# Depthwise convolution taps moved from TensorE to ScalarE and GpSimd in a two-layer decoder trunk

## What is computed

```
u = h @ w_in + b_in                       # 2048 -> 4096
a, gate = split(u)
u = a * sigmoid(gate)
u = causal depthwise convolution of u, 31 taps per channel, + b_dw
u = silu(layer_norm(u, ln_g, ln_b))
return u @ w_out + b_out
```

## Time and profile before

| | us |
|---|---|
| median of 3 runs | 2216.86 (2216.32 to 2218.45) |
| the profiled execution's own time | 2215.75 |
| its span in the trace | 2214.0 |
| TensorE busy | 2192.6 (99%) |
| VectorE busy | 1417.3 (64%) |
| ScalarE busy | 1006.6 (45%) |
| GpSimd busy | 208.1 (9%) |
| mean granted TensorE clock | 0.998 |

### The profile page before, as it was taken

The page is one execution under the profiler, slowest core; times in us unless marked ns, Lnnn a source line. Parts: engine busy times, 40 slices in busy tenths (PEclk is TensorE's granted clock), DMA queues, the critical chain, the costliest instruction groups (busy, mean ns, idle before and its releaser), DMA issues.

```text
span 2214.0 us, 32918 instructions
## 1 busy us (share of the span) xinstructions
PE 2192.6 (99%) x13136; PEld 1945.1 (88%) x13136; DVE 1417.3 (64%) x1319; ACT 1006.6 (45%) x890; POOL 208.1 (9%) x125
## 2 busy tenths in 40 slices
PE   8999899999999999999999999999999999999998
PEld 8999788888888888888888898888888888888887
DVE  7999877555555554556767667775565556555655
ACT  7665645443344433444444444444443344433444
POOL 7999100000000000000000000000000000000000
PEclk9999999999999999999999999999999999999999
DMA  9665354546554555455454435555555554555462
GB/s 238 169 175 166 117 207 171 209 171 209 189 190 171 208 189 196 171 209 190 172 172 142 143 115 204 186 204 175 202 173 206 175 204 174 206 190 190 172 212 77
DMA packets 250048, 400.54 MB, mean 181 GB/s; under 512 B 6407, under 2 KB 72143, under 8 KB 249935
## 3 DMA queue, kind: packets, MB, share of 16 engines
q1 hardware_dynamic: 249406, 398.74, 53.3%
q0 software_dynamic: 352, 0.56, 0.1%
q10 hardware_dynamic: 208, 0.07, 0.0%
HBM read 397.24 MB, written 2.10 MB: 180 GB/s over the span
## 4 chain that ended last, share of the span: by engine, by line
PE 89%; DVE 6%; issue 2%; DVEq 1%; DMA 0%; POOL 0%; ACT 0%; SPq 0%; ACTq 0%; POOLq 0%
PE bank L1317 54%; PE bank L1319 28%; DVE bank L980 4%; PE bank L1618 4%; PE bank L1603 1%; PE bank L1680 1%; PE bank L1414 0%; DVEq L979 0%; DMA x_rows<-in_x 0%; DVE bank L991 0%; DVE u L961 0%; DVE bank L988 0%; DVE act L942 0%; PE bank L1417 0%; PE bank L1550 0%
## 5 line engine op out<-in xcount | busy, mean ns | idle before, releaser
L1317 PE MATMUL bank<-x_both,w_hi 128*128 128x512 f32 x3328 | 1155.9, 393 | 0.0
L843 DVE TENSOR_TENSOR w_lo<-raw,w_hi 128x2048 fp32r<-128x2048 f32 x343 | 779.0, 2289 | 528.3 <-ACT w_hi L529 528.1
L529 ACT ACTIVATE w_hi<-raw 128x2048 fp32r<-128x2048 f32 x374 | 707.6, 1910 | 627.7 <-PE bank L1319 601.1
L1319 PE MATMUL bank<-x_both,w_lo 128*128 128x256 f32 x3328 | 927.0, 279 | 0.0
L1317 PEld LDWEIGHTS bank<-x_both,w_hi 128*128 128x128 f32 x3328 | 623.3, 187 | 141.4 <-issue 0.3
L1317 PE MATMUL bank<-h_both,w_hi 128*128 128x512 f32 x1872 | 651.1, 393 | 0.4 <-DVE h_both L1026 0.4
L1319 PEld LDWEIGHTS bank<-x_both,w_lo 128*128 128x128 f32 x3328 | 627.0, 188 | 0.1
L1319 PE MATMUL bank<-h_both,w_lo 128*128 128x256 f32 x1872 | 521.6, 279 | 0.0
L1317 PEld LDWEIGHTS bank<-h_both,w_hi 128*128 128x128 f32 x1872 | 350.8, 187 | 81.0 <-issue 0.5
L1319 PEld LDWEIGHTS bank<-h_both,w_lo 128*128 128x128 f32 x1872 | 352.6, 188 | 0.0
L1400 PE MATMUL bank<-x_both,w_hi 128*128 128x256 f32 x960 | 173.5, 283 | 0.0
(11 more groups left out here) (230 smaller groups left out, 1271.7 us busy)
## 6 DMA issues: line engine op xcount, KB each, us to landing
raw<-in_ffn_w_gate_up SPq DMA_DIRECT2D x176, 1024.0 KB, 4.9
raw<-in_ffn_w_down SPq DMA_DIRECT2D x88, 1024.0 KB, 5.1
raw<-in_gla_w_in SPq DMA_DIRECT2D x48, 1024.0 KB, 5.2
raw<-in_conv_w_in SPq DMA_DIRECT2D x32, 1024.0 KB, 6.0
raw<-in_conv_w_out SPq DMA_DIRECT2D x16, 1024.0 KB, 5.1
raw<-in_gla_w_out SPq DMA_DIRECT2D x16, 1024.0 KB, 6.6
x_rows<-in_x SPq DMA_DIRECT2D x4, 512.0 KB, 6.4
out<-out_rows SPq DMA_DIRECT2D x4, 512.0 KB, 3.1
```

What stands on the lines that cost most here:

```text
L529: nc.scalar.activation(w_hi[k][:, :, :], raw[k][:, :, :], ACT.Copy).then_inc(hi_done, 1)
L843: nc.vector.tensor_tensor(w_lo[k][:, :, :], raw[k][:, :, :], w_hi[k][:, :, :].bitcast(F32), ALU.subtract).then_inc(lo_done, 1)
L1317: mm(to, w_hi[k][:, kt, cols], xx[:, :, k0 + kt, :], start=(first and kt == 0), stop=False, skip_group_check=True)
L1319: ins = mm(to[:, 0:T], w_lo[k][:, kt, cols], xx[:, 0, k0 + kt, :], start=False, stop=(last and kt == 3), skip_group_check=True)
```

## The change

- **TensorE has no taps in tiles 0 to 13.** `conv_taps`, its diagonals, the split of u and of the tap weights go. ScalarE makes six products a tile instead of four.
- **The six products.** The first, with the bias, is written into PSUM (`tap_first`) and is the addend of VectorE's first tap. Four go to `tap_four`; GpSimd adds two of them onto the other two in one instruction of 512 columns (`add_four`). The last is `tap_last`. VectorE adds the two folded ones and the last in three single-width steps at positions 13 to 15 (`ADD_AT`), 9 to 11 in tile 15. Each product counts on one semaphore.
- **u is made ahead.** `gated` for the next tile stands at step 16 of the present one (`NEXT_U_AT`).
- **Join.** The last step but one of a tile writes its accumulator into `act`; one join at step 4 of the next tile is left.
- **The last two tiles.** 4 and 14 taps are made by TensorE after all products, in full float32 with plain diagonals of ident and u, into banks that the products have left (`y_last`); `join_last` adds them.
- **Squares.** The squares of tiles 0 to 7 get a place of their own, are made while ScalarE handles tile 14, and GpSimd adds them ahead of the last fold. Two sums that GpSimd made go to TensorE.
- **Shift.** One shift matmul instead of two.

```diff
-PE_TAPS = 2
-ACT_TAPS = 4
-MORE_TAPS = (2, 10)
-TAP_STEPS = DVE_TAPS + 2
-JOIN_AT = 6
+ACT_TAPS = 6
+LAST_TAPS = (4, 14)
+DVE_TAPS = TAPS - ACT_TAPS
+TAP_STEPS = DVE_TAPS + 3
+JOIN_AT = 4
+ADD_AT = 13
+NEXT_U_AT = 16
...
+        shift_bank = pair_s[1][:, T:2 * T]
+        tap_first = pair_s[0][:, 0:T]
+        y_last = [slot[1][:, 2, :], slot[1][:, 0, :]]
...
 # GpSimd
+            def add_four(tile):
+                pool.wait_ge(product_done, ACT_TAPS * tile + 5)
+                nc.gpsimd.tensor_tensor(tap_four[:, 0:2, :], tap_four[:, 0:2, :], tap_four[:, 2:4, :], ALU.add).then_inc(four_added, 1)
...
-                    split_u(2 * i + (2 + t), t)
-                    sum_pair(2 * i + (2 + t))
+                    if last and t == 1:
+                        pool.wait_ge(y_sq, 2)
+                        nc.gpsimd.tensor_tensor(sq_early[:, 0:4, :], sq_early[:, 0:4, :], sq_early[:, 4:8, :],
+                                                ALU.add).then_inc(sq_pre, 1)
+                    add_four(2 * i + (2 + t))
...
 # ScalarE, conv_turn
-                        diagonals(2 * i + t, t)
-                        hi(i + (j + 1) // RING, (j + 1) % RING)
+                    hi(i + (j + 1) // RING, (j + 1) % RING)
+                    if last and t == 0:
+                        square_tiles(sq_early[:, 0:4, :], 0, 4, first_shifted, 4)
+                        square_tiles(sq_early[:, 4:8, :], 4, 8, join_done, 8)
                     scalar.wait_ge(acc_read[t], U_CONV_IN // 2 + 1 + i)
-                    nc.scalar.activation(u_hi[:, t, :], u[:, t, 0:UW], ACT.Copy).then_inc(uhi_done, 1)
+                    product(0, tap_first, ACT.Identity, bias=vec[:, ds(VCOL["conv_b_dw"] + tile, 1)])
+                    for n in range(4):
+                        product(1 + n, tap_four[:, n, :], ACT.Copy)
+                    product(5, tap_last[:, :], ACT.Copy)
...
             conv_turn(2)
+            last_diagonals(0)
             conv_turn(3)
+            last_diagonals(1)
...
 # VectorE
+            def gated(i, t):
...
+                dve.wait_ge(sig_done, tile + 1)
+                dve.wait_ge(w_used, 4 * i + 2 * t + 2)
+                if not first:
+                    dve.wait_ge(tap_done, TAP_STEPS * (tile - 1))
+                nc.vector.scalar_tensor_tensor(out=u[:, t, PAD:PAD + T], ...).then_inc(acc_read[t], 1)
...
+                j = on_pe
+                for n in range(TAP_STEPS - on_pe):
...
+                    if n >= 2:
+                        dve.wait_ge(tap_done, done + n - 1)
+                    if n == 0:
+                        dve.wait_ge(product_done, ACT_TAPS * tile + 1)
+                        nc.vector.scalar_tensor_tensor(out=acc, in0=tap, scalar=w, in1=tap_first,
+                                                       op0=ALU.mult, op1=ALU.add).then_inc(tap_done, 1)
...
+                    elif add_at <= n < add_at + 2:
+                        dve.wait_ge(four_added, tile + 1)
+                        nc.vector.tensor_tensor(acc, acc, tap_four[:, n - add_at, :], ALU.add).then_inc(tap_done, 1)
+                    elif n == add_at + 2:
+                        dve.wait_ge(product_done, ACT_TAPS * tile + 6)
+                        nc.vector.tensor_tensor(acc, acc, tap_last[:, :], ALU.add).then_inc(tap_done, 1)
+                    else:
+                        to = joined(tile) if n == TAP_STEPS - on_pe - 2 else acc
+                        nc.vector.scalar_tensor_tensor(out=to, in0=tap, scalar=w, in1=acc,
+                                                       op0=ALU.mult, op1=ALU.add).then_inc(tap_done, 1)
...
+                    if n == JOIN_AT and not (first and t == 0):
+                        join(tile - 1, 1 - t)
+                    if n == NEXT_U_AT and not last:
+                        gated(i + t, 1 - t)
+                    if n == JOIN_AT + 4 and last:
+                        join_last(0)
...
 # TensorE
+            def last_taps(n):
+                pe.wait_ge(acc_read[n], U_CONV_IN // 2 + KT // 2)
+                pe.wait_ge(sig_done, KT)
+                for j in range(LAST_TAPS[n]):
+                    at = n * LAST_TAPS[0] + j
+                    pe.wait_ge(diag_done, at + 1)
+                    ins = mm(y_last[n], last_diag[at][:, :], u[:, n, j:j + T], start=(j == 0), stop=(j == LAST_TAPS[n] - 1))
                 ins.then_inc(pe_taps, 1)
...
+            with pe.Fori(2, KT // 2) as i:
+                for t in range(2):
+                    conv_product(i, t)
+            last_taps(0)
+            last_taps(1)
```

More of the change, by code:

```diff
@@ L420, in _ @@
                 n += 1
[L421 to L426, removed]
             pool.wait_ge(x_t, 4)
@@ new lines, in conv_turn, with product @@
+                    if isinstance(i, int) and i == 0 and t == 0:
+                        scalar.wait_ge(par_read, 2)
+                    scalar.wait_ge(acc_read[t], U_CONV_IN // 2 + 1 + i)
+                    tile = 2 * i + t
+                    def product(n, to, func, **bias):
+                        k = TAPS - ACT_TAPS + n
+                        nc.scalar.activation(to, u[:, t, k:k + T], func, scale=dw[:, ds(TAPS * tile + k, 1)],
+                                             **bias).then_inc(product_done, 1)
@@ L956, in conv_tile @@
                 if not first:
-                    dve.wait_ge(ulo_done, tile - 1)
-                    dve.wait_ge(join_done, 2 * tile - 2)
-                if not (first and t == 0):
-                    dve.wait_ge(tap_done, done)
+                    dve.wait_ge(tap_done, TAP_STEPS * (tile - 1))
                 nc.vector.scalar_tensor_tensor(out=u[:, t, PAD:PAD + T], in0=slot[t][:, 0, :],
@@ L963, in conv_tile @@
                                                in1=gate[:, t, :], op0=ALU.add, op1=ALU.mult).then_inc(acc_read[t], 1)
+            def conv_tile(i, t, on_pe=0, fewer=0, shifted=True, add_at=ADD_AT, last=False):
+                tile = 2 * i + t
+                done = TAP_STEPS * t - fewer + 2 * TAP_STEPS * i
+                first = isinstance(i, int) and i == 0
+                if not first:
+                    dve.wait_ge(join_done, tile - 1)
                 dve.wait_ge(acc_read[t], U_CONV_IN // 2 + i + 1)
-                for n, j in enumerate(range(PE_TAPS + more, TAPS - ACT_TAPS)):
+                j = on_pe
+                for n in range(TAP_STEPS - on_pe):
@@ L981, in conv_tile @@
                                                        op0=ALU.mult, op1=ALU.add).then_inc(tap_done, 1)
-                    if join_at <= n < join_at + 2 and not (first and t == 0):
-                        join(tile - 1, 1 - t, n - join_at)
-                n = DVE_TAPS - more
-                acc = y_acc[t][:, n % 2, :]
-                dve.wait_ge(pair_sum, tile + 1)
-                dve.wait_ge(tap_done, done + (n - 1))
-                nc.vector.tensor_tensor(acc, acc, tap_sum[:, :], ALU.add).then_inc(tap_done, 1)
@@ L993, in _ @@
+            gated(0, 0)
             for i in range(2):
```

244 lines of the change are left out of this document (62 added, 182 removed).

## The result

The changed kernel takes 2198.12 us (median of 4 runs, 2196.72 to 2199.57) against 2216.8 for the kernel before beside it: a ratio of 0.9914, with a 95% interval of 0.9897 to 0.9932. Two later series gave it 2200.86 and 2200.40, against 2217.2 and 2216.46 (ratios 0.9934 and 0.9929): 18.7, 16.3 and 16.1 us less, under 1% of the whole. The forecast was 2200.0, in a range of 2197.0 to 2206.0: it was right, and so was the case behind it. The profiled execution took 2196.72 us, its span 2195.0.

The account below looks back on a forecast made before the run. VectorE was taken to pace the convolution stage, with TensorE bounding the untouched stretch behind it. An earlier last u (15.2 us) and shorter tail (1.7) sum to 16.9 less: median 2200.0 us, range 2197.0 to 2206.0.

Parts of the forecast that it names:

- A VectorE tile: Convolution stage: 25 taps, three adds, one join and one u sum to 11.52 us; 11.70 with loop holes, ends 11.52 and 12.0.
- the hole of the turn: VectorE's idle place at the loop's turn every second tile: taken as 0.35 us a turn, 0.18 a tile.
- The first step at 0.39: VectorE's first tap of a tile, addend in PSUM: 0.39 us, against the skill's 0.065 more each, 1.0 over sixteen.
- The start: First tiles, following TensorE's products: u of tile 1 at 44.45 us, tile 4 at 79.5; then VectorE slower, tile 15 at 208.1.
- The fold: GpSimd's add of ScalarE's products: done at worst 8.1 us after u, needed at 9.8, so VectorE never waits.
- Rival 3: GpSimd's fold comes too late, VectorE stalls 3.7 us on every tile: 2252 us, slower than before; chance 0.04.
- fourteen diagonals at nothing: ScalarE's diagonals for the last taps, 7 us once, fit its idle share: cost nothing, or some 2 us without cover.
- The tail: Last u to variance: 11.5 us against 13.21, 1.7 less; join at 10.2, square 0.5, TensorE's add 0.59, with hand-overs 1.3.
- Released by ScalarE's last square: Sign expected in the changed profile's tail: the variance about 11.5 us after the last u, released by that square.
- The sum: Whole kernel: u of tile 15 earlier by 15.2 us plus a tail shorter by 1.7 make 16.9 less.
- Rival 1: TensorE paces the convolution stage throughout, hiding the loop's turn: u of tile 15 at 206.3, 2198.7 us; chance 0.13.
- Rival 2: Costlier register work, 12.1 a tile, and TensorE's clock falls: u of tile 15 at 212.1, tail 12.8, 2205.3 us; chance 0.12.

## Why the prediction was right, point by point

- **A VectorE tile, 11.52 without holes, 11.70 with:** 11.51 and 11.64 in the nine tiles. The sum by steps of 0.39 was right to 0.01, u included; the hole of the turn was 0.29 in place of 0.35.
- **The first step at 0.39 with its addend in PSUM:** L909 lasts 0.48 and is followed 0.40 later, like a step. The 1.0 us over sixteen of them that would follow from the Trainium skill (VectorE: DVE Perf Modes, the section on the TRN2 errata) isn't there. The reason given, two rows of 479 and 478 ns, was right but thin: what speaks for PSUM is the 8.0 us that the sixteen steps last longer with their addend in SBUF, which the prediction had no term for and no row of before could show. That the choice of PSUM was worth 7.7 us was luck as far as the prediction goes.
- **The start:** u of tile 1 at 44.68 (44.45), of tile 4 at 79.65 (79.5), tile 14 at 196.11 (196.5), tile 15 at 207.62 (208.1).
- **The fold, 8.1 behind u against 9.8:** in tile 8 it ended at 135.00, 8.8 behind u, and the adds came at 136.62, 10.4 behind u: room of 1.6, as forecast, with both ends 0.6 to 0.7 later. Tile 0, where two remainders stood ahead (40.31 against 33.69), waited 1.60, and this hid behind u's wait for TensorE. Rival 3 was cut down rightly, and its fixed stall "on every tile" is not how it would have gone: with the adds eight steps earlier there were two waits in sixteen tiles.
- **ScalarE, and fourteen diagonals at nothing:** the first product lasts 0.57 and brings no table load. The diagonals took 4.19 (117.72 to 121.91) and delayed a weight copy, GpSimd waited 2.15 for it at 123.79, and no one waited for GpSimd.
- **The tail, 11.5:** 11.88. The term that was mis-sized is the 1.3 for square, sum and hand-overs: VectorE joined at 217.79, 10.2 behind u as forecast, and the variance came 1.71 later. The square's sum had ended at 218.99; what ended later, at 219.45, is the second of VectorE's own two short steps behind the sum of the values (218.58 and 219.03, each taking its predecessor's result). The forecast had no term for them. "Released by ScalarE's last square" was wrong with it. TensorE had the sums ahead of the last join done 9.9 behind u and not 9.5, and idled 0.32 there.
- **The sum, 16.9 earlier:** 16.97 at the variance. That it fits to 0.1 is luck: u of tile 15 came 0.4 earlier than the sum had it and the tail was 0.4 longer. The profile came out at 2196.72 rather than 2198.9 because of the 2 us in the stretch behind, which belong to the execution; the median of later runs, 2200.4 to 2200.9, is the better match to the 2200.0.
- **Rival 1** (TensorE paces throughout, 2198.7) is nearer to the first median of 2198.12 than the forecast, by its number. Its mechanism isn't there: it had u of tile 15 at 206.3, and it needs VectorE to wait for TensorE ahead of u in tile after tile, where the view of waits names TensorE once, at tile 1.
- **Rival 2** (12.1 a tile, then a fallen clock: u of tile 15 at 212.1, tail 12.8) was never this kernel, but one step more makes it: 212.47 and 13.45. The fall of the clock came with it, and the tail was 0.65 us longer than the rival had it.

## What to carry to other kernels

Where VectorE and GpSimd both work without a pause, look at where VectorE's operands lie: a tensor-scalar from SBUF to SBUF, 0.34 us when nothing was in its way, lasted up to 3.84 in the rows above, a step with both inputs in SBUF up to 2.31, and the steps above with one operand in PSUM lasted the same in every tile. The profile shows the loss as a longer instruction on VectorE and not as a wait. When one engine's product begins another's chain, make what it is computed from well ahead: a dozen steps here, and without that one instruction's place the gain was gone. After a balanced stage, 5 us of waiting ahead of TensorE's last work cost the fallen clock besides: a tail of 13.45 in place of 11.88.

## What the runs showed of the hardware

- VectorE beside GpSimd: a scalar-tensor-tensor with two SBUF inputs and an output in PSUM ended 0.28 to 0.31 behind GpSimd's instruction in flight (11 of 11); a tensor-scalar from SBUF to SBUF 0.14 to 0.16 behind it (14 of 14); a scalar-tensor-tensor with one SBUF and one PSUM input and an SBUF output never waited (16 of 16 at 0.47 to 0.48), nor did a tensor-scalar from SBUF into PSUM (16 of 16 at 0.55).
- That tensor-scalar, when free, lasted 0.34, where the same operation into PSUM lasts 0.48.
- TensorE's granted clock went to the 1.2 GHz level during an idle stretch of 5.02 us ahead of its last work (0.58 in 210 to 214, 0.56 in the next 4 us), and shortly behind one of 4.00 us (0.50 in 221 to 224, with the matmul that ended the stretch at 219.75).
- At a granted clock of 1.00 and a busy share of 100%, the same matmuls ran at one of two paces, 577 or 566 in 100 us, by execution.
